# A decoder layer on one core: the first modulation and the first ten units of the input projection, by chunks of 128 features

## The chip, the core and the metric

The kernel runs on one core of a Trainium2 chip, as one launch. Its time is the device time in microseconds, and the number to compare is the median of several executions. The engines are TensorE (PE), VectorE (DVE), ScalarE (ACT), GpSimd (POOL) and SyncE (SP); PEld is TensorE's weight load. The work of each engine is written out by hand, and the engines wait for each other on semaphores.

## What is computed

One layer over 256 tokens of 1024 features. A vector c gives six modulation rows, of which the first two (shift and scale) act on the normalised input:

```python
mod = silu(c) @ w_ada + b_ada                   # w_ada: 1024 x 6144
sh1, sc1, g1, sh2, sc2, g2 = split(mod, 6)
h = rms_norm(x, g_pre_mix) * (1.0 + sc1) + sh1
proj = h @ w_in                                 # queries, keys, values of three attentions, index heads, gates
y = merge(attention_sb, attention_moba, attention_dsa, gates) @ w_o
x = x + g1 * rms_norm(y, g_post_mix)
h = rms_norm(x, g_pre_ffn) * (1.0 + sc2) + sh2
x = x + g2 * rms_norm((silu(gate) * up) @ w_down, g_post_ffn)
```

Products with weights are done as three products of a high and a low part, so each weight and each h is cut in two: high part by ScalarE, the rest by VectorE.

## The kernel before

**Blocks and units.** w_in is loaded in blocks of columns (`MIX_BLOCKS`) into two buffers `raw`, cut into `whi` and `wlo` (`cut_hi` L625, `cut_lo`, its line L923), and multiplied by units: a unit is one tile of 128 output columns, or of one half of the tokens for value blocks. There are 51 units (`mix_units` L73). Units 0 to 9 belong to blocks 0 to 3: index keys with weights, four tiles of index queries, two of queries and two of keys of the second attention, and the last heads of both. Units 10 and 11 are its values, 12 to 17 queries and keys of the first attention, 18 and 19 its values, 20 to 26 the third attention, 27 to 50 the gates. A unit runs over the 8 chunks of 128 features with three matmuls each (`three`, L1259 to L1261), into one of two PSUM banks, and ScalarE copies it out (`take_unit` L682).

**The first modulation.** SyncE loads c, x, the bias and gain vectors, and then the first 2048 columns of w_ada in six transfers with 8 KB in a row. `first_products` multiplies them chunk by chunk with silu(c) (L1266). VectorE copies the rows out (L1005), TensorE turns them (L1299), VectorE makes the shift and scale columns (L975, L979). x has been scaled by its inverse root and turned meanwhile (L1316); VectorE and ScalarE modulate it, chunk by chunk, and cut it (L1030, L733, L737, L1038). Only then unit 0 starts.

**What else is hung on the units.** All engines walk the same list of units in the same order. At unit u, VectorE does the low parts of the next block (`PIECES_AT`), index logits, parts of the softmax, rounds of the top-k search (units 25 to 32), and at the units in `ADA_UNIT` one of 16 steps of the second and third modulation: GpSimd loads 1 MB of w_ada into `ada_part`, which lies in the buffer of the modulated x, and VectorE adds it, times a column of silu(c), to `acc` (`accumulate`, L999; L993 and L996 for the first of eight). GpSimd loads part n+1 once VectorE is through with part n (`load_part` L542); there is one buffer. Head n of the 16 is scored behind unit `HEAD_START` + 2n, exponentiated one unit later, normalised by VectorE at the next, and turned or summed by TensorE behind the third. Index logits are made in pairs of heads behind units 5, 7, 9 and 11. GpSimd masks the scores once all are added.

## Time and profile before

| | us |
|---|---|
| median of three runs | 473.8 (473.58 to 475.11) |
| profiled execution | 475.17 |
| its span | 473.0 |

| engine | busy us | share |
|---|---|---|
| TensorE | 441.7 | 93% |
| VectorE | 317.1 | 67% |
| ScalarE | 237.7 | 50% |
| GpSimd | 55.0 | 12% |

The span is the stretch from the first to the last instruction of one execution; its time is that of the whole launch, 2.2 us more. Times in rows are from the span's start. A row of a timeline gives start, duration, engine, line, operation, output and inputs, shapes and count; in brackets is the idle time of the engine before it and who ended it. Matmuls overlap in a pipeline: the distance between starts tells their pace, not the duration.

### The profile page before, as it was taken

Reading aid. Unit: us, or ns where it says so; the run is one execution under the profiler, and the core shown is the slowest. Engines: PE = TensorE matmul, PEld = TensorE weight load, DVE = VectorE, ACT = ScalarE, POOL = GpSimd, SP = SyncE. Lnnn points to the kernel's source line nnn. Section 1 sums busy time; section 2 is a strip of 40 time slices with the busy share of each in tenths; the row PEclk is TensorE's granted clock in tenths of the full one; section 3 lists DMA queues with packets and bytes.
Section 4 is the critical chain, followed back from the end, with each engine's and each line's share of the span. In section 5 each row is a group of like instructions: output and inputs, shape, how many; then the busy total and the mean of one; then the engine's idle time right before and its main releaser. Section 6 shows DMA issues by size and latency. Waiting matters only on the chain.

```text
span 473.0 us, 7656 instructions
## 1 busy us (share of the span) xinstructions
PE 441.7 (93%) x2927; PEld 389.7 (82%) x2927; DVE 317.1 (67%) x542; ACT 237.7 (50%) x417; POOL 55.0 (12%) x84
## 2 busy tenths in 40 slices
PE   0959999999999999999979999999999999999994
PEld 0529999999889989998977799888888888888883
DVE  3047678768399959673789547785855675585545
ACT  6046555647576655657547237554454253445232
POOL 2001001200023140000399100000000000000000
PEclk9958999999999999999999999999999999999998
DMA  8996888596955675742667910997475646620002
GB/s 299 424 367 212 290 303 292 178 307 216 346 184 187 254 267 187 268 156 81 202 214 276 372 72 2 327 361 265 143 236 177 190 165 204 236 93 1 1 0 89
DMA packets 56817, 99.85 MB, mean 211 GB/s; under 512 B 5212, under 2 KB 41684, under 8 KB 53716
## 3 DMA queue, kind: packets, MB, share of 16 engines
q1 hardware_dynamic: 54132, 81.62, 50.4%
q0 software_dynamic: 2656, 17.84, 10.7%
q8 instruction: 19, 0.31, 0.3%
q14 instruction: 10, 0.08, 0.0%
HBM read 98.39 MB, written 1.06 MB: 210 GB/s over the span
## 4 chain that ended last, share of the span: by engine, by line
PE 88%; DMA 4%; DVE 3%; issue 2%; ACT 1%; SPq 1%; DVEq 0%; ACTq 0%; PEldq 0%
PE psum L1259 19%; PE psum L1260 17%; PE psum L1261 17%; PE psum L1559 16%; PE psum L1560 8%; DMA ada_end<-in_w_ada_dram 4%; PE psum L1523 3%; PE psum L1410 1%; PE psum L1349 1%; PE psum L1347 1%; PE psum L1381 1%; DVE wlo L923 1%; PE psum L1392 1%; PE psum L1316 1%; DVE acc L999 0%
## 5 line engine op out<-in xcount | busy, mean ns | idle before, releaser
L1559 PE MATMUL psum<-hcut,whi 128*128 128x512 f32 x320 | 111.7, 394 | 0.0
L1259 PE MATMUL psum<-hcut,whi 128*128 128x256 f32 (+1 forms) x360 | 106.3, 295 | 3.2 <-DVE hcut L1038 2.7
L1260 PE MATMUL psum<-hcut,whi 128*128 128x256 f32 (+1 forms) x360 | 102.9, 286 | 0.0
L1261 PE MATMUL psum<-hcut,wlo 128*128 128x256 f32 (+1 forms) x360 | 102.9, 286 | 0.0
L923 DVE TENSOR_TENSOR wlo<-raw,whi 128x1024 fp32r<-128x1024 f32 (+4 forms) x84 | 78.9, 967 | 24.9 <-ACT whi L634 24.6
L1560 PE MATMUL psum<-hcut,wlo 128*128 128x256 f32 x320 | 88.8, 277 | 0.0
L1259 PEld LDWEIGHTS psum<-hcut,whi 128*128 128x128 f32 (+1 forms) x360 | 69.4, 193 | 8.0 <-issue 3.2
L634 ACT ACTIVATE whi<-raw 128x1024 fp32r<-128x1024 f32 (+4 forms) x84 | 66.3, 821 | 16.5 <-DMA raw<-in_w_in_dram 16.5
L1559 PEld LDWEIGHTS psum<-hcut,whi 128*128 128x128 f32 x320 | 60.0, 188 | 14.1 <-issue 0.2
L1260 PEld LDWEIGHTS psum<-hcut,whi 128*128 128x128 f32 (+1 forms) x360 | 69.4, 193 | 0.0
L1261 PEld LDWEIGHTS psum<-hcut,wlo 128*128 128x128 f32 (+1 forms) x360 | 69.3, 192 | 0.0
L1560 PEld LDWEIGHTS psum<-hcut,wlo 128*128 128x128 f32 x320 | 60.1, 188 | 0.4
L1188 DVE TENSOR_TENSOR dlo<-draw,dhi 128x2048 fp32r<-128x2048 f32 x11 | 25.1, 2292 | 43.7 <-ACT dhi L832 43.7
L1183 DVE TENSOR_TENSOR wlo<-raw,whi 128x1024 fp32r<-128x1024 f32 x40 | 47.1, 1221 | 4.6 <-ACT whi L825 4.6
L825 ACT ACTIVATE whi<-raw 128x1024 fp32r<-128x1024 f32 x40 | 39.8, 1046 | 3.2 <-DMA raw<-in_w_up_dram 3.2
L832 ACT ACTIVATE dhi<-draw 128x2048 fp32r<-128x2048 f32 x11 | 20.9, 1912 | 30.8 <-PE psum L1261 30.8
L999 DVE SCALAR_TENSOR_TENSOR acc<-xn,csil,acc 128x2048 f32<-128x2048 f32 x14 | 32.9, 2350 | 4.9 <-DMA xn<-in_w_ada_dram 4.8
L870 ACT ACTIVATE fsil<-fsil 128x256 f32<-128x256 f32 x20 | 8.4, 418 | 52.8 <-DVE fsil L1200 52.8
L1260 PE MATMUL psum<-dlo,fhi 128*128 128x512 f32 x88 | 34.3, 390 | 0.0
L1259 PE MATMUL psum<-dhi,fhi 128*128 128x512 f32 x88 | 34.3, 390 | 0.0
L1261 PE MATMUL psum<-dhi,flo 128*128 128x512 f32 x88 | 34.3, 390 | 0.0
L1260 PE MATMUL psum<-wlo,hcut 128*128 128x320 f32 (+2 forms) x80 | 27.8, 347 | 0.0
(180 smaller groups left out, 695.7 us busy)
## 6 DMA issues: line engine op xcount, KB each, us to landing
raw<-in_w_up_dram SPq DMA_DIRECT2D x22, 1024.0 KB, 7.6
xn<-in_w_ada_dram POOLq DMA_DIRECT2D x16, 1024.0 KB, 5.2
raw<-in_w_in_dram SPq DMA_DIRECT2D x7, 2048.0 KB, 8.5
draw<-in_w_down_dram SPq DMA_DIRECT2D x11, 1024.0 KB, 5.0
raw<-in_w_in_dram SPq DMA_DIRECT2D x4, 1280.0 KB, 6.7
raw<-in_w_in_dram SPq DMA_DIRECT2D x3, 1536.0 KB, 6.9
raw<-in_w_ada_dram SPq DMA_DIRECT2D x2, 2048.0 KB, 9.7
ada_end<-in_w_ada_dram SPq DMA_DIRECT2D x4, 1024.0 KB, 16.9
```

The lines of the kernel that those rows point to most:

```text
L634: act.activation(block_view(whi[b % 2], b)[0:p, chunks, cols], block_view(raw[r % 2], b)[0:p, chunks, cols], ACT.Copy).then_inc(w_hi, 1)
L825: act.activation(block_view(whi[slot], B_FFN)[:, 2 * q:2 * q + 2, :], block_view(raw[slot], B_FFN)[:, 2 * q:2 * q + 2, :], ACT.Copy).then_ ...
L832: act.activation(dhi[slot][:, :, :], draw[slot][:, :, :], ACT.Copy).then_inc(d_hi, 1)
L923: dve.tensor_tensor(block_view(wlo[b % 2], b)[0:p, chunks, cols], block_view(raw[r % 2], b)[0:p, chunks, cols], block_view(whi[b % 2], b)[ ...
L999: ins = dve.scalar_tensor_tensor(acc[:, :], ada_part, csil[:, k:k + 1], acc[:, :], ALU.mult, ALU.add)
L1183: dve.tensor_tensor(block_view(wlo[slot], B_FFN)[:, 2 * q:2 * q + 2, :], block_view(raw[slot], B_FFN)[:, 2 * q:2 * q + 2, :], block_view(w ...
L1188: dve.tensor_tensor(dlo[slot][:, :, :], draw[slot][:, :, :], dhi[slot][:, :, :].bitcast(F32), ALU.subtract).then_inc(d_lo, 1)
L1259: pe.matmul(dst, a[0], b[0], start=first, stop=False)
L1260: pe.matmul(dst, a[0], b[1], start=False, stop=False)
L1261: return pe.matmul(dst, a[1], b[0], start=False, stop=last)
L1559: pe.matmul(dst[:, :], wh, hcut[:, k, :, :].rearrange("p a s -> p (a s)"), start=k == 0, stop=False)
L1560: mm = pe.matmul(dst[:, S:2 * S], wl, hhi[:, k, :], start=False, stop=k == KC - 1)
```

## The change

The first modulation is computed for one chunk of 128 features at a time, and each chunk's part of units 0 to 9 follows at once. For chunk k SyncE loads the shift and scale columns of that chunk from all rows of w_ada (two transfers, 512 bytes in a row, into one of three buffers) and the chunk's 128 rows of the 1224 columns of blocks 0 to 3 (three transfers). `row_products` makes the modulation row of the chunk, ScalarE copies it, `turn_row` turns it into two columns, VectorE adds bias and gain, multiplies the raw transposed x by scale and inverse root, ScalarE adds the shift and cuts, VectorE makes the rest. The ten units then take three matmuls each, into ten half banks side by side, which stay open over all eight chunks. The row products of chunk k+1 stand behind the first of the ten units of chunk k, its turn behind the fourth. x is turned unscaled, by transposes; both inverse roots are computed in one chain of two columns, spread to a row and multiplied in. ScalarE takes the ten units after the last chunk. The bias and gain vectors are loaded by ScalarE's queue. From unit 10 on the old form goes on, with all four pairs of index logits behind units 10 to 13, heads one unit later (`HEAD_START` 14) and the sixteen steps of the later modulation at other units.

```diff
+FIRST_BLOCK, FIRST_UNIT = 4, 10
+Q_COLS, CHUNK_COLS = W_IX + HD + H_IX, W_IX + HD + H_IX + 2 * W_MB
+CHUNK_BASE = [W_IX, 0, Q_COLS, Q_COLS + W_MB - HD]
...
-HEAD_START = 13
+HEAD_START = 14
...
+LOGIT_PAIR_AT = {FIRST_UNIT + j: j for j in range(H_IX // 2)}
...
-ADA_UNIT = [2, 4, 6, 9, 12, 15, 18, 22, 25, 28, 31, 34, 37, 40, 43, 46]
+ADA_UNIT = [11, 13, 15, 17, 19, 21, 23, 25, 27, 30, 32, 34, 37, 40, 43, 46]
...
+        ada = [sb(f"ada{i}", [P, KC, 2, P], scope=start) for i in range(3)]
+        end_raw, end_hi, end_lo = [[sb(f"end_{name}{i}", [P, CHUNK_COLS], dt, scope=start) for i in range(2)]
+                                   for name, dt in (("raw", F32), ("hi", F32R), ("lo", F32R))]
...
+        def chunk_view(bufs, ends, k):
+            if k >= 6:
+                return ends[k - 6][:, :]
+            return bufs[k // 3][:, CHUNK_COLS * (k % 3):CHUNK_COLS * (k % 3 + 1)]
+        def first_place(u):
+            return bank[u // 2][:, S * (u % 2):S * (u % 2 + 1)]
+        def mod_turned_col(k):
+            return bank[6 + k % 2][:, 2 * k:2 * k + 2]
...
+            def load_chunk(k):
+                if k >= 3:
+                    sp.wait_ge(gemv, k - 2)
+                for a in range(2):
+                    sp.dma_start(ada[k % 3][:, :, a, :], ada_dram[:, :, D * a + P * k:D * a + P * (k + 1)]).then_inc(ada_in[k], 16)
+                view = chunk_view(raw, end_raw, k)
+                sp.dma_start(view[:, 0:Q_COLS], in_dram[:, k, O_QIX:O_QIX + Q_COLS]).then_inc(chunk_in[k], 16)
+                heads = in_dram[:, k, O_QMB:O_QMB + 2 * W_MB].rearrange("p (a n) -> p a n", a=2)
+                pairs, last = view[:, Q_COLS:CHUNK_COLS - P], view[:, CHUNK_COLS - P:CHUNK_COLS]
+                sp.dma_start(pairs.rearrange("p (a n) -> p a n", a=2), heads[:, :, 0:W_MB - HD]).then_inc(chunk_in[k], 16)
+                sp.dma_start(last.rearrange("p (a n) -> p a n", a=2), heads[:, :, W_MB - HD:W_MB]).then_inc(chunk_in[k], 16)
+            def load(b):
+                dst, arrived = raw[b % 2], raw_in[b % 2]
+                if b < FIRST_BLOCK + 2:
+                    sp.wait_ge(w_hi, 6 * (b - FIRST_BLOCK + 1))
+                    sp.wait_ge(w_lo, 6 * (b - FIRST_BLOCK + 1))
+                else:
+                    sp.wait_ge(w_hi, 4 * (b - 1))
+                    sp.wait_ge(w_lo, 4 * (b - 1))
...
-                    pool.wait_ge(h_lo, 4)
+                    pool.wait_ge(tmp_ready, KC)
...
+            for k in range(KC):
+                act.wait_ge(chunk_in[k], 48)
+                act.activation(chunk_view(whi, end_hi, k), chunk_view(raw, end_raw, k), ACT.Copy).then_inc(w_hi, 2)
+                act.wait_ge(gemv, k + 1)
+                if k >= 2:
+                    act.wait_ge(mod_turned, k - 1)
+                act.activation(mrow[:, S * (k % 2):S * (k % 2 + 1)], bank[5][:, 0:S], ACT.Copy).then_inc(row_kept, 1)
+                act.wait_ge(tmp_ready, k + 1)
+                act.activation(hhi[:, k, :], htmp[k % 2], ACT.Identity, bias=col[0][:, k:k + 1]).then_inc(chunk_hi, 1)
+                if k == 1:
+                    act.preload_act_table_set("natural_log_exp_and_others")
             for q in range(4):
...
+                cut_hi(FIRST_BLOCK, q)
...
+            for u in range(FIRST_UNIT):
+                take_unit(u)
+            for u in range(FIRST_UNIT, N_UNITS):
...
+            v2, r2, t2 = var[:, 0:TT], rinv[:, 0:TT], root_[:, 0:TT]
+            then(dve.reciprocal(r2, t2))
+            then(dve.tensor_tensor(t2, v2, r2, ALU.mult))
+            then(dve.tensor_tensor(t2, t2, r2, ALU.mult))
+            then(dve.tensor_scalar(t2, t2, -0.5, 1.5, ALU.mult, ALU.add))
+            dve.tensor_tensor(r2, r2, t2, ALU.mult).then_inc(root_ready, 1)
+            dve.wait_ge(root_turned, 1)
+            dve.tensor_copy(rootrow, bank[3][:, S:2 * S]).then_inc(rootrow_ready, 1)
+            def chunk_cut_lo(k):
+                dve.wait_ge(w_hi, 2 * (k + 1))
+                dve.tensor_tensor(chunk_view(wlo, end_lo, k), chunk_view(raw, end_raw, k),
+                                  chunk_view(whi, end_hi, k).bitcast(F32), ALU.subtract).then_inc(w_lo, 2)
+            def chunk_columns(k):
+                dve.wait_ge(mod_turned, k + 1)
+                shift, scale = mod_turned_col(k)[:, 0:1], mod_turned_col(k)[:, 1:2]
+                then(dve.scalar_tensor_tensor(col[0][:, KC + k:KC + k + 1], scale, vecs[:, VEC_ADA + KC + k:VEC_ADA + KC + k + 1],
+                                              vecs[:, VEC_PRE_MIX + k:VEC_PRE_MIX + k + 1], ALU.add, ALU.mult))
+                then(dve.tensor_tensor(col[0][:, k:k + 1], shift, vecs[:, VEC_ADA + k:VEC_ADA + k + 1], ALU.add))
+                dve.sem_inc(mod_ready, 1)
+                if k == 0:
+                    dve.wait_ge(rootrow_ready, 1)
+                if k % 4 < 2:
+                    dve.wait_ge(x_kept_act, k // 4 + 1)
+                else:
+                    dve.wait_ge(x_kept_dve, k // 4 + 1)
+                if k >= 2:
+                    dve.wait_ge(chunk_hi, k - 1)
+                dve.scalar_tensor_tensor(htmp[k % 2], h32[:, k, :], col[0][:, KC + k:KC + k + 1], rootrow,
+                                         ALU.mult, ALU.mult).then_inc(tmp_ready, 1)
+            def chunk_rest(k):
+                dve.wait_ge(chunk_hi, k + 1)
+                dve.scalar_tensor_tensor(hlo[:, k, :], htmp[k % 2], col[0][:, k:k + 1], hhi[:, k, :].bitcast(F32),
+                                         ALU.add, ALU.subtract).then_inc(chunk_lo, 1)
+            for k in range(KC):
+                if k:
+                    chunk_cut_lo(k)
+                chunk_columns(k)
+                if k == 0:
+                    chunk_cut_lo(0)
+                chunk_rest(k)
+            dve.sem_inc(col_ready, 1)
             for q in range(4):
...
+                cut_lo(FIRST_BLOCK, q)
...
+            def row_products(k):
+                pe.wait_ge(ada_in[k], 32)
+                if k == 0:
+                    pe.wait_ge(c_ready, 2)
+                else:
+                    pe.wait_ge(row_kept, k)
+                w = ada[k % 3]
+                for half in range(2):
+                    for j in range(4):
+                        mm = pe.matmul(bank[5][32 * j:32 * j + 32, 0:S], crep[:, 4 * half + j, :],
+                                       w[:, 4 * half + j, :, :].rearrange("p a n -> p (a n)"),
+                                       start=half == 0, stop=half == 1, tile_position=(0, 32 * j))
+                mm.then_inc(gemv, 1)
...
+            def turn_row(k):
+                pe.wait_ge(row_kept, k + 1)
+                if k == 0:
+                    pe.wait_ge(pick_ready, 1)
+                if k < 2:
+                    pe.wait_ge(x_kept_dve, 1)
+                else:
+                    pe.wait_ge(mod_ready, k - 1)
+                if k == 0:
+                    pe.wait_ge(x_kept_act, 1)
+                for a in range(2):
+                    mm = pe.matmul(mod_turned_col(k)[:, a:a + 1], mrow[:, S * (k % 2) + P * a:S * (k % 2) + P * (a + 1)], pick[:, :],
+                                   start=True, stop=True)
+                mm.then_inc(mod_turned, 1)
+            def turn_raw_x(i):
+                for t in range(TT):
+                    if i == 0:
+                        pe.wait_ge(x_in[t], 16)
+                    for c in (2 * i, 2 * i + 1):
+                        mm = pe.transpose(turned(c)[:, P * t:P * (t + 1)], xt[:, t, P * c:P * (c + 1)], ident[:, :])
+                mm.then_inc(x_raw_turned, 1)
+            def first_unit(u, k):
+                b, what, c0, n, dest = UNITS[u]
+                base = CHUNK_COLS - P if what == "last head" else CHUNK_BASE[b] + c0
+                wh, wl = [chunk_view(x, ends, k)[:, base:base + n] for x, ends in ((whi, end_hi), (wlo, end_lo))]
+                dst = first_place(u)[0:n, :]
+                pe.matmul(dst, wh, hhi[:, k, :], start=k == 0 and u in (1, 2, 4, 6, 8), stop=False, skip_group_check=True)
+                pe.matmul(dst, wh, hlo[:, k, :], start=False, stop=False, skip_group_check=True)
+                return pe.matmul(dst, wl, hhi[:, k, :], start=False, stop=k == KC - 1, skip_group_check=True)
...
+            for i in range(4):
+                turn_raw_x(i)
             pe.wait_ge(vec_in, 16 * 6)
-            pe.transpose(bank[0][:, 0:VEC_END], vec_rows[:, :], ident[0:VEC_END, 0:VEC_END]).then_inc(vec_turned, 1)
+            pe.transpose(bank[4][:, 0:VEC_END], vec_rows[:, :], ident[0:VEC_END, 0:VEC_END]).then_inc(vec_turned, 1)
+            row_products(0)
+            pe.wait_ge(root_ready, 1)
             for t in range(TT):
-                turn_x(0, t)
-            first_products()
-            turn_rows(0)
-            for u in range(N_UNITS):
+                mm = pe.transpose(bank[3][:, S + P * t:S + P * (t + 1)], rinv[:, t:t + 1].to_broadcast([P, P]), ident[:, :])
+            mm.then_inc(root_turned, 1)
+            turn_row(0)
+            for k in range(KC):
+                pe.wait_ge(w_hi, 2 * (k + 1))
+                pe.wait_ge(w_lo, 2 * (k + 1))
+                pe.wait_ge(chunk_hi, k + 1)
+                pe.wait_ge(chunk_lo, k + 1)
+                for n in range(FIRST_UNIT):
+                    u = n ^ 1 if k == 0 and n < 2 else n
+                    if k == 0 and n == 0:
+                        pe.wait_ge(x_kept_act, 2)
+                    if k == 0 and u == 2:
+                        pe.wait_ge(x_kept_dve, 2)
+                    if k == 0 and u == 6:
+                        pe.wait_ge(rootrow_ready, 1)
+                    if k == 0 and u == 8:
+                        pe.wait_ge(vec_ready, 1)
+                    mm = first_unit(u, k)
+                    if k == KC - 1:
+                        mm.then_inc(units, 1)
+                    if n == 0 and k < KC - 1:
+                        row_products(k + 1)
+                    if n == 3 and k < KC - 1:
+                        turn_row(k + 1)
+                if k < KC - 1:
+                    mm.then_inc(chunk_done, 1)
+            for u in range(FIRST_UNIT, N_UNITS):
```

## Rows read from the trace of the kernel before

**Rows 1.** page, part 1: busy us, share of the span, instructions

```profile
PE 441.7 (93%) x2927; PEld 389.7 (82%) x2927; DVE 317.1 (67%) x542; ACT 237.7 (50%) x417; POOL 55.0 (12%) x84
```

**Rows 2.** timeline of the start, all engines

```profile
6.11 0.63 ACT L648 ACTIVATE xn<-xt 128x512 f32<-128x512 f32 x1 [0.59 <-DMA xt<-in_x_dram]
...
27.01 1.94 PE L1266 MATMUL psum<-ada_end,crep 128*32 128x512 f32 x8 [1.57 <-DMA ada_end<-in_w_ada_dram]
...
29.85 1.11 PE L1299 MATMUL psum<-ident,mrow 128*128 128x128 f32 x4 [0.91 <-DVE mrow L1005]
...
33.66 0.46 PE L1259 MATMUL psum<-hcut,whi 128*72 128x256 f32 x1 [2.70 <-DVE hcut L1038]
```

**Rows 3.** stretches: length, busy (instructions) per engine, granted clock, DMA share, GB/s

```profile
15.00:20.00 5.00, 5.00 (x46) 3.08 (x49) 0.00 (x0) 0.00 (x0) 0.00 (x0) 1.00 1.01 428
36.00:38.00 2.00, 2.00 (x12) 2.00 (x11) 1.57 (x2) 2.00 (x4) 0.69 (x1) 0.50 0.04 13
39.00:40.00 1.00, 1.00 (x9) 1.00 (x8) 1.00 (x2) 1.00 (x2) 0.00 (x0) 0.74 0.70 246
150.00:160.00 10.00, 10.00 (x82) 9.43 (x81) 9.82 (x20) 6.21 (x10) 2.84 (x8) 1.00 0.87 304
```

**Rows 4.** timeline of TensorE: products, first unit, logits, end of the tenth unit

```profile
17.30 3.64 PE L1266 MATMUL psum<-raw,crep 128*32 128x512 f32 x32
...
34.14 0.41 PE L1261 MATMUL psum<-hcut,wlo 128*72 128x256 f32 x1
...
34.35 0.41 PE L1259 MATMUL psum<-hcut,whi 128*72 128x256 f32 x1
...
54.02 0.49 PE L1347 MATMUL psum<-qk 64*128 64x128 f32 x4
...
54.87 0.38 PE L1259 MATMUL psum<-hcut,whi 128*128 128x256 f32 x1
...
67.62 0.49 PE L1347 MATMUL psum<-qk 64*128 64x128 f32 x4
```

**Rows 5.** DMA packets, at 47 to 48, then at 45 to 46.5

```profile
DMA packets 938, 0.31 MB, mean 311 GB/s; under 512 B 912, under 2 KB 931, under 8 KB 931
...
q1 hardware_dynamic: 931, 0.25, 119.4%
...
DMA packets 462, 0.59 MB, mean 394 GB/s; under 512 B 0, under 2 KB 462, under 8 KB 462
```

**Rows 6.** groups of instructions by form: count, busy us, mean ns, idle before

```profile
L634 ACT ACTIVATE whi<-raw 128x1024 fp32r<-128x1024 f32 x28 | 28.9, 1050 | 0.0
...
L812 ACT ACTIVATE hcut<-xn 128x256 fp32r<-128x256 f32 x8 | 3.3, 418 | 14.6 <-POOL xn L607 14.6
...
L1064 DVE SCALAR_TENSOR_TENSOR score<-bufp,wix,score 128x256 f32<-128x256 f32 x7 | 3.4, 480 | 0.0
...
L1523 PE MATMUL psum<-xn,raw 128*128 128x128 f32 x128 | 14.7, 276 | 0.7 <-ACT xn L665 0.7
```

**Rows 7.** parts of the later modulation: landing, issue, sum; GpSimd's mask

```profile
DMA to landing us min/median/max: 4.9/5.2/7.3
...
55.34 0.53 POOL L548 DMA_DIRECT2D xn<-in_w_ada_dram  x1 [9.44 <-DVE acc L999]
...
60.28 2.35 DVE L999 SCALAR_TENSOR_TENSOR acc<-xn,csil,acc 128x2048 f32<-128x2048 f32 x1 [0.59 <-DMA xn<-in_w_ada_dram]
...
81.42 3.23 POOL L566 TENSOR_SCALAR_AFFINE_SELECT score<-score 128x128 f32<-128x128 f32 x2 [8.48 <-DVE score L1064]
```

**Rows 8.** timeline: takes of units 17 and 27, VectorE between

```profile
95.48 0.38 ACT L697 ACTIVATE qk<-psum 128x256 f32<-128x256 f32 x1 [0.83 <-PE psum L1261]
...
127.28 0.56 DVE L1095 SCALAR_TENSOR_TENSOR bufp<-psum,bufa 128x384 f32<-128x384 f32 x1 [4.68 <-ACT bufa L754]
...
129.40 2.36 DVE L923 TENSOR_TENSOR wlo<-raw,whi 128x1024 fp32r<-128x1024 f32 x2 [0.97 <-ACT whi L634]
...
137.80 0.47 ACT L706 ACTIVATE qk<-psum,vecs 128x256 f32<-128x256 f32 x1 [1.38 <-PE psum L1261]
```

More of the change, by code:

```diff
@@ L88, in mix_units @@
     features(2, T_QMB, W_MB - HD)
-    keys(3, T_QMB, T_KMB, W_MB)
+    features(3, T_KMB, W_MB - HD)
+    units.append((3, "last head", W_MB - HD, P, (T_QMB + W_MB // P, T_KMB + W_MB // P)))
     tokens(4, "values", 0, W_MB, V_MB)
@@ L181, in pieces_at @@
     plan = {}
-    for b in range(N_MIX):
+    for b in range(FIRST_BLOCK, N_MIX):
         us = [n for n, u in enumerate(UNITS) if u[0] == b]
@@ L210 @@
     0, 3 * KC, 9 * KC, 10 * KC, 11 * KC, 12 * KC, 13 * KC)
-SIGMOID_FROM = max(EXP_AT) + 4
+SIGMOID_FROM = max(EXP_AT) + 3
 EARLY_GATES = SIGMOID_FROM - FIRST_GATE
 SIGMOID_BATCHES = 3
-def raw_uses():
-    uses = [("ada", u) for u in range(2)]
-    uses += [("block", b) for b in range(B_FFN)]
-    return uses
-RAW = raw_uses()
-N_RAW = len(RAW)
+N_RAW = B_FFN - FIRST_BLOCK
 LOADS = {b: 1 for b in range(B_FFN)}
@@ L232, in raw_arrivals @@
 def raw_arrivals():
-    count, out = [0, 0], []
-    for r, (kind, b) in enumerate(RAW):
-        count[r % 2] += 16 * (1 if kind == "ada" else LOADS[b])
-        out.append(count[r % 2])
+    count, out = [0, 0], {}
+    for b in range(FIRST_BLOCK, B_FFN):
+        count[b % 2] += 16 * LOADS[b]
+        out[b] = count[b % 2]
     return out, count
 RAW_ARRIVED, RAW_COUNT = raw_arrivals()
-RAW_OF_BLOCK = {b: r for r, (kind, b) in enumerate(RAW) if kind == "block"}
 def decoder_layer(nc, x, c, w_ada, b_ada, g_pre_mix, g_post_mix, w_in, b_gate, w_proj_sb,
@@ L560, in _ @@
             load_part(0)
[L561 to L562 removed]
+            for u in range(FIRST_UNIT, N_UNITS):
+                if u == max(LOGIT_PAIR_AT):
                     pool.wait_ge(score_added, TT * H_IX)
@@ L683, in take_unit @@
                 b, what, c0, n, dest = UNITS[u]
-                src = bank[B_UNIT + u % 2]
-                act.wait_ge(units, u + 1)
+                src = first_place(u) if u < FIRST_UNIT else bank[B_UNIT + u % 2]
+                act.wait_ge(units, 2 * (u // 2) + 2 if u < FIRST_UNIT else u + 1)
                 if what == "index keys and weights":
@@ L731, in _ @@
-            for pair in range(4):
-                c = 2 * pair
-                act.activation(h32[:, c, :], turned(c), ACT.Identity, bias=col[0][:, c:c + 1],
-                               scale=col[0][:, 8 + c:9 + c]).then_inc(h_act, 1)
-                act.wait_ge(h_act, pair + 1)
-                act.wait_ge(h_dve, pair + 1)
-                act.activation(hhi[:, 2 * pair:2 * pair + 2, :], h32[:, 2 * pair:2 * pair + 2, :], ACT.Copy).then_inc(h_hi, 1)
-            for u in range(N_UNITS):
+            act.wait_ge(x_in[0], 16)
@@ L1024, in _ @@
[L1024 to L1039 removed]
+            dve.wait_ge(ident_ready, 1)
@@ new lines, in _ @@
+            dve.tensor_reduce(pick[:, :], ident[:, :].rearrange("p (a b) -> p a b", b=32)[:, :, 0], AX_X, ALU.add).then_inc(pick_ready, 1)
+            dve.wait_ge(x_in[1], 16)
+            dve.tensor_tensor_reduce(squares0[1], xt[:, 1, :], xt[:, 1, :], 1.0, 0.0, ALU.mult, ALU.add,
+                                     ssq[:, 0, 1:2]).then_inc(ss_ready, 2)
+            for i in (1, 3):
+                dve.wait_ge(x_raw_turned, i + 1)
+                dve.tensor_copy(h32[:, 2 * i:2 * i + 2, :], turned_two(i)).then_inc(x_kept_dve, 1)
@@ new lines, in _ @@
+            dve.wait_ge(vec_turned, 1)
+            then(dve.tensor_copy(vecs[:, :], bank[4][:, 0:VEC_END]))
+            dve.wait_ge(ss_ready, 4)
+            then(dve.tensor_scalar(var[:, 0:TT], ssq[:, 0, :], 1.0 / D, EPS, ALU.mult, ALU.add))
+            dve.sem_inc(var_ready, 2)
+            then(dve.tensor_scalar(vecs[:, VEC_ADA + KC:VEC_ADA + 2 * KC], vecs[:, VEC_ADA + KC:VEC_ADA + 2 * KC], 1.0, None, ALU.add))
+            dve.sem_inc(vec_ready, 1)
+            dve.wait_ge(sqrt_ready, 2)
```

256 lines of the change are left out of this document (96 added, 160 removed).

## The prediction

> **What bounds the kernel now.** Read the busy shares first: TensorE is busy 93% of the span, VectorE 67% [rows 1]. Then the timeline of the start, because the change is there: x has landed at 6.11, the last products of the first modulation end at 28.95, waiting for their weights, and the first unit's matmul starts only at 33.66 [rows 2]. Until then the DMA engines run without a gap (428 GB/s, share 1.01 at 15 to 20 us [rows 3]), so the first 29 us are bound by 8 MB of modulation weights, and 4.7 us more by a serial chain. From 33.66 on TensorE has almost no idle time until the merge. So a microsecond of unit work moved ahead of 33.66 is a microsecond won, unless TensorE must then wait for someone later.
>
> **The reference point.** Units 0 to 9 are the same in both kernels. In before the tenth ends at 67.62 [rows 4], with two of four pairs of index logits already done by then (units 5 and 7). A pair costs 54.87 - 54.02 = 0.85, with its restart 0.9. Without them and 0.2 for two small transposes the ten units would end at 67.6 - 1.8 - 0.2 = 65.6. In after, all logits come behind the tenth unit. The question is when that end comes.
>
> **Start of after.** x is in at about 6.1. Sixteen raw transposes of x (0.23 each by the four at 29.85 [rows 2]) take until about 9.8, the vectors' transpose follows. Sums of squares and root: now one chain for both token tiles, some eight tiny operations at 0.2 behind the copies of x; I put it at 10 to 12, its two transposes and the copy at 13. The load of chunk 0 is 1.05 MB of modulation weights and 0.63 MB of w_in. The trace has no 512-byte packets in bulk: 256-byte ones (nearly all of the 931 on queue 1 at 47 to 48) move 0.25 MB in about 0.9 us, 280 GB/s, those of 1280 bytes 394 [rows 5]. In time per packet 512 bytes lie nearer the small ones; I take 325, ends 280 and 394. A chunk is then 3.2 + 1.7 = 4.9 us (ends 4.3 and 5.5); chunk 0 lands near 11.0, chunk 7 near 45.5 (ends 41 and 50). Behind chunk 0: ScalarE's cut of 1224 columns at 1050 ns per 1024 is 1.25 [rows 6], the row's copy 0.35, turn 0.6, columns 0.5, product 0.48; then VectorE's low part of the chunk (two of 1024 columns take 2.36 [rows 8]), 1.45, and of h, 0.45 [rows 6]. 11.0 + 5.3 = 16.3 for TensorE's first unit matmul.
>
> **The chunk loop.** Per chunk 30 matmuls at 0.12 (82 in the 10 us at 150 to 160 [rows 3]) = 3.6; 8 x 3.6 = 28.8. They are before's own matmuls: nothing is added. Added in between, 7 times: the row products of the next chunk (in before 32 records take 3.64 [rows 4] and eight make one of the eight rows of products, so 0.9; after has half the columns and twice the records per eighth, the same streaming) and turn_row, four records at 115 ns (14.7 us for 128) and a wait, 0.6 [rows 6]. In before these products lie under the DMA and cost nothing; here they stand in TensorE's order: 7 x 1.5 = 10.5. Clock: in before TensorE is at its 1.2 GHz level from the sparse stretch before 33.66 until about 39.5 (0.50 granted at 36 to 38, 0.74 in the second at 39; spacing 0.21, from 34.14 to 34.35, against 0.12 [rows 3, 4]). After 10 us with little work (11 to 16) I expect the same again, 5.8 us at half speed = 2.9. Sum: 16.3 + 28.8 + 10.5 + 2.9 = 58.5.
>
> Does anything else set the chunk's period of 5.1? DMA, 4.9, runs ahead and isn't late even at its upper end. ScalarE has 2.0, VectorE 2.9 per chunk. The serial chain after turn_row (columns 0.45, product 0.48, ScalarE's bias and cut 0.42, VectorE's rest 0.45, four hand-overs of 0.05 to 0.15) is 2.1 to 2.3 against 2.2 of units 4 to 9 that cover it. It just about fits; I add 1.1 over the loop (ends 0 and 5). The table load at chunk 1 fits in ScalarE's slack. **End of the tenth unit: 59.6, that is 6.0 earlier** (ends 1 and 9: no cold clock and an early start on one side, 0.7 per chunk of slip on the other).
>
> **Behind the loop: what gives it back.** SyncE's loads of blocks 4 and 5 are queued behind chunk 7 and land before 57, the takes of ten units (12 ScalarE operations, 4.5 us) run beside units 10 and 11, whose waits need only banks 0 and 1. Logits in pairs at 10 to 13 are the same work as before. I cost these at 0; uncovered, the takes could cost 2.
>
> Not free is the later modulation. In before sixteen parts of 1 MB are taken up at units 2, 4, 6, 9, 12, 15, 18, 22, every three units; in after only from unit 11, every second one: 11, 13, ..., 27. There is one buffer, so a part's cycle is: 2.35 for the sum on VectorE, 0.3 until GpSimd's issue, 5.2 to landing (min 4.9, max 7.3): 7.85; the pair 55.34 to 60.28 shows it with VectorE waiting for the DMA [rows 7]. Two feature units take TensorE 48 x 0.12 = 5.8 plus attention, some 7.2 where no value units lie. VectorE works in order: what is queued behind the waiting sum are softmax norms and low parts of the weights, and TensorE waits for both.
>
> Walk it, with T the end of the tenth unit. At unit 13 VectorE is through the logits at T+18.7, GpSimd masks the scores first (3.23 us [rows 7]) and issues part 2 at T+22.1; it lands at T+27.3. VectorE reaches it at T+24.5 and waits. Its norm of head 0, behind it, comes at T+31.3, while TensorE is ready for that head's transposes, behind unit 17, at T+29.75 (two value units at 3.5 by their 320 columns, six feature units at 3.0, four logit pairs, a score pair): 1.6 lost. Parts 3 to 6 follow every 7.85, part 7 behind the first top-k round, its sum ending at T+69.8; the third piece of the first gate block then is ready at T+70.9, against T+67.0 when TensorE reaches it unhindered (the ten units 18 to 27 take 95.4 to 137.7 in before [rows 8], less 1.4 for the sum over parts and 1.6 for heads that come later in after, and 1.5 before the unit's end): 3.9 lost, the first 1.6 in it. With 0.2 for the fourth piece: **4.1 back.** Price per us of landing time: about 5 us, as five landings stand in a row. From unit 27 on VectorE is full (9.82 of 10 us at 150 to 160 [rows 3]) and has 3 us more to do up to unit 34 than before; but it starts block 11's low part some 6 earlier than 129.40 [rows 8], so this costs nothing more. From unit 35 on both kernels are alike but for the heads one unit later; with the last output at unit 49 of 50, I put it at 0 (ends -0.5 and +1).
>
> **Sum:** 6.0 - 4.1 = 1.9 saved. Against the profiled execution (475.17, span 473.0, 2.2 outside it) 473.3; the median shown, 473.8, is 1.4 below that execution, so 471.9.
>
> **Rivals.** *A, the parts come late.* Queue 1's blocks and the parts share the DMA engines; in after they collide more often. For it: the landing of 7.3 in before. Against: 5.2 in the median. At 6.3 on average for five landings: 5 x 1.1 = 5.5 more, 477.4. The mechanism is VectorE's wait for part_in ahead of the norms; it decides from a landing of 5.6 (1.9 / 5 above 5.2) to slower than before. *B, nothing is given back.* If VectorE's lag is hidden (TensorE needs a piece only when it reaches it), the six stay: 467.8. For it: VectorE idles 4.68 us before 127.28 in before [rows 8]. *C, the chunk loop is slower than the sum:* transfers of 512 bytes at 200 GB/s would make 7.0 per chunk, chunk 7 landing at 60 and the tenth unit at 68: 473.8 + 8.4 - 6.0 + 4.1 = 480.3. For it speaks nothing in rows 5. *D, a cold loop:* if TensorE waits in each chunk and the granted clock stays at 0.50, as it did at 36 to 38, the loop costs 8 x 3.6 more less the 2.9 counted, 26 us: near 498. The Trainium skill (TensorE: Matmul & The Clock Gate, HAM oscillation) describes just such loops over K tiles, in which the wait for each tile throttles the engine anew. Against it: the sum above leaves hardly any wait inside the loop; 0.03.
>
> **Chances.** Forecast (470 to 474) 0.5; A 0.27; B 0.15; C and others of the loop 0.05; D 0.03. About 0.3% (1.4 us) can be told from no change: so faster is B, 0.28 of the forecast's half and a little of C's opposite, 0.45; same 0.31; slower 0.24. Range for 8 in 10: 467.8 to 477.8; the forecast's own is 470 to 474.
>
> **What would show it.** First unit matmul at 15 to 18 (before 33.66); 0.50 granted there for about 6 us; ten matmul groups per chunk at a period of 5.1 to 5.4; tenth unit's end at 58 to 61. VectorE waiting for DMA of xn at units 15 to 23, 2 to 3 us each; TensorE idle before a p transpose (L1392's like) at unit 17 and before the first gate block. Wrong if the row products wait for ada, if VectorE shows no wait for xn (then B), or if the span before the tenth unit's end is over 64.

## The result and the profile after

The changed kernel takes 489.55 us (median of 4 runs, 486.49 to 491.51) against 474.46 (4 runs, 473.58 to 475.17): ratio 1.0307, 95% interval 1.028 to 1.0333. It is slower by some 15 us; the forecast was 471.9 in a range of 467.8 to 477.8. The profiled execution is the fastest of the four, 486.49 with a span of 484.8, so the two profiles differ by 11.8 us in span, and the profile accounts for that much of the 15. The other three show a mean granted clock of 0.975 to 0.981 instead of 0.995.

Page of after, busy time per engine: the shares are those of before [rows 1] within 1%. TensorE's busy time is 7.8 us longer, VectorE's 6.1; the shares alone don't tell where.

```profile
PE 449.5 (93%) x3005; PEld 392.7 (81%) x3005; DVE 323.2 (67%) x554; ACT 238.7 (49%) x412; POOL 52.8 (11%) x84
```

The timeline of the start of after (start, duration, engine, line, operation, idle time and its releaser):

```profile
11.11 1.93 PE L1341 MATMUL psum<-ada,crep 128*32 128x256 f32 x16 [1.05 <-DMA ada<-in_w_ada_dram]
13.03 1.22 ACT L758 ACTIVATE whi<-raw 128x1224 fp32r<-128x1224 f32 x1 [1.69 <-DMA raw<-in_w_in_dram]
18.75 0.55 PE L1377 MATMUL psum<-hcut,whi 128*128 128x256 f32 x1 [3.15 <-DVE hcut L1095]
19.10 0.42 PE L1378 MATMUL psum<-hcut,whi 128*128 128x256 f32 x1
19.31 0.41 PE L1379 MATMUL psum<-hcut,wlo 128*128 128x256 f32 x1
...
22.02 0.40 PE L1379 MATMUL psum<-hcut,wlo 128*72 128x256 f32 x1
22.24 0.31 PE L1377 MATMUL psum<-hcut,whi 128*128 128x256 f32 x1
...
22.50 0.28 PE L1379 MATMUL psum<-hcut,wlo 128*128 128x256 f32 x1
22.62 0.28 PE L1377 MATMUL psum<-hcut,whi 128*128 128x256 f32 x1
```

First unit matmul at 18.75 (before 33.66 [rows 2]). The stretches of this profile give a granted clock of 1.00 from 18 us on, but the pace doesn't agree: the matmuls start 0.21 apart until 22.24, which is before's spacing at the 1.2 GHz level [rows 4], and 0.12 apart from then on. So the first 3.5 us of the units ran at half clock here too. Then the inside of one chunk, and the last matmul of the tenth unit with the first of the eleventh:

```profile
36.24 0.48 DVE L1095 SCALAR_TENSOR_TENSOR hcut<-bufp,col,hcut 128x256 fp32r<-128x256 f32 x1 [0.58 <-ACT hcut L764]
37.35 1.07 PE L1341 MATMUL psum<-ada,crep 128*32 128x256 f32 x16
...
39.52 0.50 PE L1358 MATMUL psum<-pick,mrow 128*128 128x1 f32 x4
41.75 0.48 DVE L1095 SCALAR_TENSOR_TENSOR hcut<-bufp,col,hcut 128x256 fp32r<-128x256 f32 x1 [0.58 <-ACT hcut L764]
41.98 0.28 PE L1379 MATMUL psum<-hcut,wlo 128*128 128x256 f32 x1
42.38 0.31 PE L1377 MATMUL psum<-hcut,whi 128*72 128x256 f32 x1
...
62.34 0.28 PE L1379 MATMUL psum<-hcut,end_lo 128*128 128x256 f32 x1
62.46 0.31 PE L1327 MATMUL psum<-whi,hcut 128*128 128x320 f32 x1
```

From 36.24 to 41.75 is the chunk's period, 5.5 us. Between two chunks (41.98 to 42.38) the next matmul comes 0.40 later instead of 0.12: TensorE takes it up when VectorE's rest of h is through, at 41.75 + 0.48. The tenth unit ends at 62.5, 3.1 earlier than the 65.6 that stand for it in before; unit 17 is taken at 92.42 (before 95.48 [rows 8]), still 3.1 ahead. Where TensorE then stands idle, by the lines that it waits at:

```profile
93.90 0.55 PE L1482 MATMUL psum<-ident,bufp 128*128 128x128 f32 x3 [1.51 <-DVE bufp L1150]
111.58 0.31 PEld L1482 LDWEIGHTS psum<-ident,bufp 128*128 128x128 f32 x3 [0.87 <-DVE bufp L1150]
128.73 0.39 PE L1327 MATMUL psum<-whi,hcut 128*128 128x320 f32 x1 [2.01 <-DVE wlo L955]
137.44 0.36 PE L1327 MATMUL psum<-hcut,whi 128*128 128x256 f32 x1 [2.31 <-DVE wlo L955]
147.50 0.42 PEld L1396 LDWEIGHTS psum<-ident,mrow 128*128 128x128 f32 x4 [1.01 <-DVE mrow L1034]
172.45 0.65 PE L1500 MATMUL psum<-buft,v 128*64 128x256 f32 x4 [1.28 <-POOL buft L602]
189.37 0.65 PE L1500 MATMUL psum<-buft,v 128*64 128x256 f32 x4 [1.59 <-POOL buft L602]
```

VectorE's norm of a head (L1150) comes late behind units 17 and 21, its low parts of the last value block and of the first gate block (L955) in units 25 and 27; the turn of a group's sum stands behind 28, GpSimd's masks (L602) behind 34 and 38. What VectorE itself waited for, and the clock behind the stall at 137 (columns: length, TensorE's busy time, granted clock, DMA share, GB/s):

```profile
89.96 2.35 DVE L1028 SCALAR_TENSOR_TENSOR acc<-xn,csil,acc 128x2048 f32<-128x2048 f32 x1 [1.94 <-DMA xn<-in_w_ada_dram]
...
116.80 0.53 POOL L576 DMA_DIRECT2D xn<-in_w_ada_dram  x1 [7.17 <-DVE acc L1028]
125.49 2.35 DVE L1028 SCALAR_TENSOR_TENSOR acc<-xn,csil,acc 128x2048 f32<-128x2048 f32 x1 [5.37 <-DMA xn<-in_w_ada_dram]
125.65 2.00 ACT L662 ACTIVATE whi<-raw 128x1024 fp32r<-128x1024 f32 x2 [2.11 <-DMA raw<-in_w_in_dram]
```

```profile
136.00:138.00 2.00, 0.56 (x5) 1.00 1.25 406
138.00:140.00 2.00, 1.81 (x10) 0.58 0.82 304
140.00:142.00 2.00, 2.00 (x10) 0.56 0.94 313
142.00:144.00 2.00, 2.00 (x11) 1.00 1.02 374
```

A part issued at 116.80 lands only at 125.49, 8.7 us later, while 2 MB of w_in (ScalarE's wait at 125.65) come over the same engines. And behind a stall of 2.5 us TensorE runs at the 1.2 GHz level for some 3.4 us: 1.7 us more.

The balance of the two profiles closes at the first projection matmul, which comes 10.2 later:

```profile
234.16 0.36 PE L1327 MATMUL psum<-ohi,whi 128*128 128x256 f32 x1 [0.90 <-issue]
```

(before: 223.96). Stalls of TensorE in after, each with its weight load's wait (the 0.4 is at 138.54, right behind the one at 137.44): 1.7 + 0.9 + 2.25 + 2.5 + 0.4 + 1.0 + 1.45 + 1.75 = 11.9; half clock 1.7; less before's own one, 0.65 at 182.82; less the lead of 3.1: 9.9 of the 10.2. Behind it 0.3 comes back up to the feed-forward loop, and 1.8 are lost in it. SyncE's issues there, one step apart, first before, then after:

```profile
349.89 0.37 SPq L507 DMA_DIRECT2D draw<-in_w_down_dram  x1
366.47 0.37 SPq L507 DMA_DIRECT2D draw<-in_w_down_dram  x1
```

```profile
343.24 0.37 SPq L534 DMA_DIRECT2D draw<-in_w_down_dram  x1
360.02 0.37 SPq L534 DMA_DIRECT2D draw<-in_w_down_dram  x1
```

16.58 against 16.78 in these two; over a pair of steps 33.13 against 33.58, in a loop whose code is the same.

### The profile page after: what moved, and what is told of

The parts are those of the page before. It is cut to its first block, busy times and chain, and to the rows that moved or that the text cites. A ratio compares the mean times of both kernels' runs of the same rounds, so it can differ in the third digit from the quotient of the medians.

```text
span 484.8 us, 7882 instructions
## 1 busy us (share of the span) xinstructions
PE 449.5 (93%) x3005; PEld 392.7 (81%) x3005; DVE 323.2 (67%) x554; ACT 238.7 (49%) x412; POOL 52.8 (11%) x84
## 4 chain that ended last, share of the span: by engine, by line
PE 70%; DVE 11%; DMA 10%; issue 4%; ACT 3%; SPq 1%; POOL 1%; DVEq 0%; ACTq 0%
PE psum L1676 15%; PE psum L1327 11%; PE psum L1329 11%; PE psum L1328 11%; DMA xn<-in_w_ada_dram 9%; PE psum L1677 8%; DVE acc L1028 4%; PE psum L1640 3%; PE psum L1377 2%; DVE wlo L955 1%; PE psum L1341 1%; DMA raw<-in_w_in_dram 1%; PE psum L1378 1%; PE psum L1379 1%; PE psum L1500 1%
## 5 line engine op out<-in xcount | busy, mean ns | idle before, releaser
L1676 PE MATMUL psum<-hcut,whi 128*128 128x512 f32 x320 | 113.3, 398 | 0.0
L1677 PE MATMUL psum<-hcut,wlo 128*128 128x256 f32 x320 | 89.8, 281 | 0.0
L1327 PE MATMUL psum<-hcut,whi 128*128 128x256 f32 x280 | 82.7, 295 | 2.5 <-DVE wlo L955 2.5
L1328 PE MATMUL psum<-hcut,whi 128*128 128x256 f32 x280 | 79.4, 283 | 0.0
L1329 PE MATMUL psum<-hcut,wlo 128*128 128x256 f32 x280 | 79.4, 283 | 0.0
L955 DVE TENSOR_TENSOR wlo<-raw,whi 128x768 fp32r<-128x768 f32 (+3 forms) x68 | 66.7, 1007 | 16.5 <-ACT whi L662 16.2
L1676 PEld LDWEIGHTS psum<-hcut,whi 128*128 128x128 f32 x320 | 60.1, 188 | 14.7
L1677 PEld LDWEIGHTS psum<-hcut,wlo 128*128 128x128 f32 x320 | 60.4, 189 | 0.3
L1327 PEld LDWEIGHTS psum<-hcut,whi 128*128 128x128 f32 x280 | 53.7, 192 | 7.8 <-issue 3.4
L662 ACT ACTIVATE whi<-raw 128x768 fp32r<-128x768 f32 (+3 forms) x68 | 55.6, 848 | 6.0 <-DMA raw<-in_w_in_dram 6.0
L1328 PEld LDWEIGHTS psum<-hcut,whi 128*128 128x128 f32 x280 | 53.8, 192 | 0.0
L1329 PEld LDWEIGHTS psum<-hcut,wlo 128*128 128x128 f32 x280 | 53.7, 192 | 0.0
L1327 PE MATMUL psum<-whi,hcut 128*128 128x320 f32 (+2 forms) x72 | 25.3, 351 | 3.5 <-DVE wlo L955 2.0
```

The source lines that it names most:

```text
L662: act.activation(block_view(whi[b % 2], b)[0:p, chunks, cols], block_view(raw[b % 2], b)[0:p, chunks, cols], ACT.Copy).then_inc(w_hi, 1)
L955: dve.tensor_tensor(block_view(wlo[b % 2], b)[0:p, chunks, cols], block_view(raw[b % 2], b)[0:p, chunks, cols], block_view(whi[b % 2], b)[ ...
L1327: pe.matmul(dst, a[0], b[0], start=first, stop=False)
L1328: pe.matmul(dst, a[0], b[1], start=False, stop=False)
L1329: return pe.matmul(dst, a[1], b[0], start=False, stop=last)
L1676: pe.matmul(dst[:, :], wh, hcut[:, k, :, :].rearrange("p a s -> p (a s)"), start=k == 0, stop=False)
```

## Experiments

All medians in us; the interval is that of the ratio to before, which read 474.3 to 475.3 beside them. Runs are called by the start of their label, x1 or z4. Runs x1, x2, x5, x6, x7 and x11 leave out part of the work, to price it.

**Parts without their bytes.** `load_part` brings 64 of 2048 columns:

```
- pool.dma_start(ada_part, ada_dram[:, n % KC, ADA_COLS * (1 + n // KC):ADA_COLS * (2 + n // KC)]).then_inc(part_in, 16)
+ c0 = ADA_COLS * (1 + n // KC)
+ pool.dma_start(ada_part[:, 0:64], ada_dram[:, n % KC, c0:c0 + 64]).then_inc(part_in, 16)
```

> The changed kernel, but each of the sixteen parts of the later modulation brings only 64 of its 2048 columns (32 KB instead of 1 MB); VectorE sums over the whole buffer as before, so most of the later modulation's weights are left out. Theory W (what is lost is VectorE's waiting for the parts, with norms and low parts queued behind it): a part lands in about 2 us, no wait is left, and the gain of the first 60 us stands: 468 to 474. Rival L (the loss lies in the chunk loop, in the takes or in GpSimd's order, not in the parts): 482 or more.

483.85 (478.89 to 484.92; 1.0089 to 1.0205). Only 5.7 of 15 us come back. That speaks against theory W as the whole cause, but the run isn't clean: its parts of 32 KB landed in 2.0 to 2.2 us with nothing else under way (issued at 59.72, 94.62, 136.79), and in 4.7 to 5.2 beside a load of w_in (86.97, 100.02, 118.18). VectorE still waited for two of them, and TensorE behind the first:

```profile
91.97 2.35 DVE L1029 SCALAR_TENSOR_TENSOR acc<-xn,csil,acc 128x2048 f32<-128x2048 f32 x1 [2.87 <-DMA xn<-in_w_ada_dram]
95.91 0.82 PE L1483 MATMUL psum<-ident,bufp 128*128 128x128 f32 x3 [1.83 <-DVE bufp L1151]
```

So 5.7 is what shorter landings give, not what no landing would.

**The same traffic, nobody waiting for it**, by a second transfer of the whole megabyte to scratch memory (x2).

> As the kernel with small parts, but behind each small part the same queue also moves the whole 1 MB into scratch memory, for which nobody waits: the traffic stays, the wait goes. Most of the later modulation's weights are left out again. Theory W: 469 to 475, near the kernel with small parts. Rival C (the traffic itself costs, by making the blocks of w_in late for ScalarE and VectorE): 479 to 488, at least half of the loss still there.

483.39 (1.0149 to 1.021), the same as without the bytes. In this form (the bytes go to memory, not to the buffer) the traffic adds nothing to the median. Here too VectorE still waited for small parts, 1.7, 1.3 and 2.9 us.

**The schedule alone, in the kernel before:**

```
- ADA_UNIT = [2, 4, 6, 9, 12, 15, 18, 22, 25, 28, 31, 34, 37, 40, 43, 46]
+ ADA_UNIT = [11, 13, 15, 17, 19, 21, 23, 25, 27, 30, 32, 34, 37, 40, 43, 46]
```

> The kernel before with one line of the change: the list of units at which the parts are taken up (11, 13, 15, ... instead of 2, 4, 6, 9, ...). Theory W: the crowding of the parts alone makes the loss, so before's start plus the same waits: 486 to 493, slower than before by 12 to 18. Rival L (the new start makes the loss): 473 to 478.

482.39 (1.0138 to 1.0172): half of the loss by one line, between the two expectations. Its profile has a stall of 1.5 us at 89.38 and one of 2 us at unit 25, with 3.4 us at half clock behind it, and its feed-forward step stays 16.55:

```profile
130.00 0.38 PE L1259 MATMUL psum<-whi,hcut 128*128 128x320 f32 x1 [2.02 <-DVE wlo L923]
```

What makes the other half (heads and logits moved, blocks met at other times) wasn't tried part by part.

**Spread evenly.**

> The changed kernel with the same sixteen parts spread evenly from unit 11 to 46 (11, 13, 16, 18, 20, 23, 25, 27, 30, 32, 34, 37, 39, 41, 44, 46), so that at most three stand two units apart in a row. Theory W: a part's cycle of 7.9 us no longer beats two and a third units of 8.7 us; a third to a half of the 13 us comes back: 482 to 486. If the loss isn't the spacing: 489 as the changed kernel.

488.44 (1.0243 to 1.0288): nearly nothing. In its profile the stalls at units 17 and 25 are gone, but there is one of 2.2 at unit 22 with 6.8 us at half clock behind it, and the one of 2.5 at unit 27 stays.

**VectorE's sums narrowed** (parts whole and waited for), and **both taken away:**

```
- ... acc[:, :], ada_part, csil[:, k:k + 1], acc[:, :], ...
+ ... acc[:, 0:64], ada_part[:, 0:64], csil[:, k:k + 1], acc[:, 0:64], ...
```

> The changed kernel with whole parts (1 MB each, waited for), but fourteen of the sixteen sums of the later modulation cover only 64 of 2048 columns, so most of the later modulation is left out. Theory V (after the kernel with small parts still took 483.9, the loss is VectorE's own work: eight sums of 2.35 us more between units 10 and 27 than the kernel before has there, and everything behind them in its order): the cycle of a part falls to 5.6 us, under two units, and VectorE is relieved: 472 to 476, no stall of over 1.5 us on TensorE between units 15 and 29, and no stretch of half clock. Rival P (late blocks of w_in, GpSimd's masks): 480 to 484.

> Small parts (64 columns, 32 KB) and sums narrowed to 64 columns in fourteen of sixteen: neither the traffic nor the work of the later modulation is left, most of it is left out. Theory V: 471 to 475, like the one with whole parts and narrow sums within 1.5 us. Then what remains against the kernel before is the first 60 us (3 us gained) and the feed-forward loop (1.9 us lost in each profile of this family). Rival P: 478 or more.

479.1 (1.0056 to 1.0131) and 476.43 (1.0009 to 1.0049), above their ranges by 3.1 and 1.4. In the first VectorE waits even longer for landings than in after (5.8, 4.7 and 5.1 us at 91.65, 106.13 and 121.76), and TensorE once behind them, at unit 17; GpSimd's masks aren't late any more, and the stall at unit 27 (2.3 with the sums) has become 0.24:

```profile
93.52 0.55 PE L1482 MATMUL psum<-ident,bufp 128*128 128x128 f32 x3 [1.44 <-DVE bufp L1150]
131.76 0.36 PE L1327 MATMUL psum<-hcut,whi 128*128 128x256 f32 x1 [0.24 <-DVE wlo L955]
```

With after this makes a square: whole 489.5; small parts 483.9 (5.7 less); small sums 479.1 (10.4 less); both 476.4 (13.1 less). So the sums, VectorE's own 2.35 us each, are the larger half, and the two overlap by 3 us. (The "eight sums more" of the expectation are four: nine stand at units 11 to 27, five in before.) (Before wasn't run without its parts: 476.4 against 474.3 isn't a price of the loop, and how much of the 10.4 the sums cost in before too isn't known.)

**What sets the chunk's period.** First less to load: from the fourth chunk on one eighth of the modulation weights. Then less for TensorE: from the third chunk on half of the row products, on top of the kernel without parts.

> The changed kernel, but from the fourth chunk on only one eighth of a chunk's modulation weights is brought (the rest of the product reads what lies in the buffer, so part of the first modulation is left out): 0.76 MB per chunk instead of 1.68. Theory D (transfers of 512 bytes and their issue set the chunk's period of 5.5 us): from chunk 3 on the period falls to the chain's own, 4.9 to 5.2, and the tenth unit ends 2 to 3 us earlier; 486 to 489. Rival S (the chain over ScalarE, VectorE and TensorE sets it): the period stays 5.4 to 5.6, the time at 489.

> Like the kernel without parts (32 KB parts, narrow sums), and from the third chunk on the row products take only the first four of eight feature groups (half of that part of the first modulation is left out): six times 0.5 us less on TensorE inside the chunk loop. Theory T (TensorE's own order of 30 matmuls, products and turn fills the chunk's 5.5 us): the period falls to 5.0 from chunk 2 on, the tenth unit ends 3 us earlier, and with VectorE relieved all of it reaches the end: 473.4 (476.4 of its own base less 3.0). Rival S (the chain over ScalarE and VectorE sets the period): 5.3 to 5.5, 475.5 to 476.5.

490.28 (1.028 to 1.0373), the low parts of h 5.5 us apart as ever (36.08, 41.59, 47.09 against 36.24, 41.75, 47.24): the DMA engines don't set it. Half the products: 474.47 against 476.43 of its base, and the same events at 35.45, 40.52, 45.60, 50.63, a period of 5.05. TensorE's own order sets it, as theory T has it, but only just: behind the turn the chain over VectorE and ScalarE ends 0.3 later than the six units that cover it, and both start from the products and the turn. The median moved 2.0 of the 3.0 expected. Theory D fell, and with it my worry about transfers of 512 bytes.

x7's profile also shows the worst case at unit 17, a part that was waited for 5.64 us and what hung on it (granted clock 0.50 from 96 to 100, half clock for 6.8 us in all):

```profile
92.86 2.35 DVE L1031 SCALAR_TENSOR_TENSOR acc<-xn,csil,acc 128x2048 f32<-128x2048 f32 x1 [5.64 <-DMA xn<-in_w_ada_dram]
96.80 0.90 PE L1485 MATMUL psum<-ident,bufp 128*128 128x128 f32 x3 [4.60 <-DVE bufp L1153]
```

**Two stalls made on purpose, in before**, ahead of units 39 and 45 (TensorE waits for short chains of GpSimd memsets).

> The kernel before with two waits put in for TensorE, ahead of units 39 and 45, on short chains of GpSimd memsets: one of about 1 us, one of about 3 us. Nothing is left out. Theory K (a long stall of TensorE is followed by a stretch of some 3.4 us at half the granted clock, a short one isn't): after the short one the granted clock stays 1.00, after the long one it is 0.50 for 3 to 4 us; 474 + 1 + 3 + 1.7 = 479.5. Rival: no such stretch, 478.

484.59 (1.0197 to 1.0233). The first came out 3.0 long instead of 1 (GpSimd was still waiting to issue a part), the second 4.0, so the short one wasn't tried. Around the first:

```profile
182.56 0.39 PE L1270 MATMUL psum<-hcut,whi 128*128 128x256 f32 x1 [3.03 <-POOLq L601]
```

```profile
182.00:184.00 2.00, 1.44 (x10) 0.86 0.70 193
184.00:186.00 2.00, 2.00 (x11) 0.50 0.96 400
186.00:188.00 2.00, 2.00 (x16) 0.79 1.05 409
```

Both are followed by some 3.4 us at half clock. By their weight loads' waits 3.3 + 4.2, and 2 x 1.7 for the clock, make 10.9; the median rose by 10.2. So theory K holds for long stalls: one of 3 us costs nearly 5. The profile has a third such stretch, from 248.3 on, behind a wait of 2.0 us that this kernel didn't add: all profiles have it in the output projection (before: 1.9 at 238.74, with 1.00 granted behind it).

**Other spacing, halves, both.** Spacing: `[10, 12, 15, 17, 20, 22, 25, 28, 31, 34, 36, ... 46]`. Halves: each part in two transfers of 1024 columns, each with its own arrival, sum and release.

> The changed kernel with the parts taken up at 10, 12, 15, 17, 20, 22, 25, 28, 31 and from 34 on every second unit: seven sums before unit 28 instead of nine, the rest where VectorE is less full (after the top-k rounds of units 25 to 32). Theory V (sums of 2.35 us and waits for landing crowd VectorE between units 15 and 29): the stalls at units 17, 19, 25 and 27 shrink from 7.7 to 2 to 3 us, the half-clock stretch at unit 28 may go with them; 480 to 484. Rival: as with the even spacing, stalls move instead of going, 487 to 490.

> The changed kernel, each part as two halves of 1024 columns with arrivals, sums and releases of their own, so that a half lands while VectorE sums the other. Same work, same bytes. Theory: the waits for landing alone are worth up to 5.6 us (489.5 against 483.9 of the kernel with small parts); two halves hide about half of them: 485 to 488. If landing isn't what matters: 489 to 491 (32 operations more on VectorE, some 2 us of it).

> The changed kernel with both: parts as two halves, and taken up at 10, 12, 15, 17, 20, 22, 25, 28, 31, 34, 36, ... 46. Alone the spacing gave 483.0, the halves 483.65, against 489.5. If crowding and landing were separate causes, 477; if both shorten the same chain of VectorE behind the same stalls (units 17 to 29), less than the sum: 479.5 to 482. Either way it stays above before's 474.4.

483.0 (1.0167 to 1.0201), 483.65 (1.0158 to 1.022), both 481.4 (1.0112 to 1.0189). They overlap, as the square said. In all three TensorE still waits at unit 27: 2.3, 2.4 and 3.1. VectorE of the kernel with both, behind ScalarE's late high part:

```profile
126.76 2.36 DVE L957 TENSOR_TENSOR wlo<-raw,whi 128x1024 fp32r<-128x1024 f32 x2 [3.12 <-ACT whi L664]
...
129.67 0.61 DVE L1191 MAX8 top<-score 128x8 f32<-128x128 f32 x2
...
131.10 2.48 DVE L1031 SCALAR_TENSOR_TENSOR acc<-xn,csil,acc 128x1024 f32<-128x1024 f32 x2
133.50 2.35 DVE L957 TENSOR_TENSOR wlo<-raw,whi 128x1024 fp32r<-128x1024 f32 x2
```

A top-k round and a sum stand between the two pairs of low parts, all in the 7 us of two value units. So the last try clears units 25 and 26 of both:

> Halves as before, and VectorE kept clear at units 25 and 26, where the low part of the first gate block falls: the parts are taken up at 10, 12, 14, 16, 18, 20, 22, then 27, 30, 33, 35, 37, 39, 42, 44, 46, the eight top-k rounds at units 27 to 34 instead of 25 to 32. Theory V: the stall of 2.5 us at unit 27 and the half-clock stretch behind it (1.7 us) go: 477 to 478.5. Rival: the stall goes to another unit, 480 to 482. In neither case under before's 474.4, since the feed-forward loop keeps its 1.9 us and the loop's gain is 3.

483.41 (480.46 to 488.11; 1.0162 to 1.0281); without the longest of the four, 1.6% above the shortest, 482.3, against 481.4 of its base. The stall at 27 is gone, and two others stand at units 21 and 22 (the expectation of x9 calls the first one unit 19), behind seven sums that are now two units apart:

```profile
112.75 0.55 PE L1485 MATMUL psum<-ident,bufp 128*128 128x128 f32 x3 [1.60 <-DVE bufp L1153]
116.85 0.36 PE L1330 MATMUL psum<-hcut,whi 128*128 128x256 f32 x1 [2.13 <-DVE wlo L957]
```

The rival was right: the stall moved. No version made here beats before.

**The feed-forward loop.** Addresses, then the place of TensorE's code: 8, 20 and 44 semaphore instructions ahead of the loop, on top of the kernel with halves and spacing, and 5 on top of the last one.

> The changed kernel with its one new small buffer made 16 columns wide instead of one (64 bytes instead of 4), which moves every buffer allocated behind it. In the kernel before a step of the feed-forward loop takes 16.55 us (the start of one load of down weights to the next), in all kernels with the change 16.80, with the same instructions. Theory A (addresses): 16.55 again, and 487.5. Rival: 16.80 and 489.5, then it is something else, the place of the loop's code for one.

> The same with 8 more semaphore instructions on TensorE ahead of the feed-forward loop, nothing else. Theory place (where TensorE's loop code lies sets its pace): a step of the loop may differ from 16.80 us in one of three kernels with 8, 20 and 44 such instructions, and comes back to 16.55 in at least one. Rival: 16.80 in all three.

> The same with 20 such instructions. Theory place: 16.55 or another step than 16.80 in at least one of the three; rival: 16.80.

> The same with 44 such instructions. Theory place: 16.55 or another step than 16.80 in at least one of the three; rival: 16.80.

> The same kernel with five more semaphore instructions on TensorE ahead of the feed-forward loop. Theory place: a step of 16.55 us in the loop; rival: 16.80 again, then the place of TensorE's code isn't shown to matter and the cause stays open. Time 477 to 479, or 1.9 less.

487.71 (1.0238 to 1.0305), and single runs of 479.65, 481.07, 486.52 and 487.85. The step is 16.76 to 16.81 in all five; x3 and x12, which are before with other edits, keep 16.55 to 16.59. Neither the one move of addresses nor any of four moves of code changes it. The cause stays open. The last profile, 4 us above the median of its base, has a head's norm late at unit 21 and nearly 14 us at half clock, from 113 to 127.

```profile
114.86 0.90 PE L1485 MATMUL psum<-ident,bufp 128*128 128x128 f32 x3 [3.85 <-DVE bufp L1153]
```

```profile
114.00:118.00 4.00, 3.14 (x15) 0.50 0.00 2
...
122.00:126.00 4.00, 4.00 (x16) 0.50 1.01 352
```

## Why the prediction was wrong

- **First unit matmul at 16.3:** 18.75. The weights of chunk 0 came at 13.03 instead of 11.0, and the chain behind them took 5.7 instead of 5.3.
- **Chunk period 5.1:** 5.5. What binds it was right (TensorE's own order, with the chain all but tied; x7 and x11 show it), one term was too small: products, turn and what lies between them are 1.9 and not 1.5 per chunk (1.07 + 0.50 in the rows, and 0.3 at the chunk's end; the 1.1 put in for that was half of it). The cold clock of 2.9 came, in half its length here: by the pace of the matmuls 3.5 us from 18.75 on, and the first chunk took 7.0, 1.5 more than the others. In x6 0.50 is granted until 27.2, and the first chunk takes 9.3. Sum: 18.75 + 7.0 + 6 x 5.5 + 3.6 = 62.4 for the 59.6 forecast. **The gain was 3.1, not 6.0.**
- **Give-back of 4.1:** this is the step that failed most. Net of before's own stall it is 11.3 in TensorE's waits and 1.7 in clock. The waits at the first head and at the gate block were foreseen by place (1.6 at unit 17, measured 1.7; 3.9 in all up to the gate block, measured 7.7); those at units 21 and 25, 3.1 together, weren't. What failed is "from unit 27 on nothing more": I argued that block 11's low part starts 6 us earlier than in before. It began at 129.48 in after, against 129.40 [rows 8]: ScalarE had waited for the block's bytes until 125.65, and VectorE for a part until 125.49. The lead was gone before the crowding began, and the crowding (low parts, top-k, sums, the group's sum and turn) then cost 2.9 at unit 27, 1.0 behind 28 and 3.2 at the masks.
- **The price was put on the wrong thing.** I priced landings, and treated a sum's own 2.35 us as already in the cycle. Of before's sums three lie at units 2 to 6, where VectorE has room, and five between units 11 and 27; after has nine there, 8.3 us more (the first of each eight takes 1.3 instead of 2.35), nearly three times its lead. The square of runs gives 10.4 to the sums and 5.7 to shorter landings; x3, the new list of units alone in before, gives 7.4 to both.
- **Rival A** had its premise nearly come true: the five parts in a row (issued at 84.97 to 116.80) land after 6.0 us on average (5.0, 5.2, 6.0, 5.0, 8.7), near the 6.3 that A names, and shorter landings give back 5.7 as against its 5.5. Yet it covers 5.5 of the 17.7 us between forecast and measurement, since it takes the same 4.1 as its base. B and C are excluded by the traces (C's 200 GB/s stands in no row; the chunks' loads moved 279 to 320); D too, the loop runs at full clock from 27 us on at the latest.
- **The clock was only counted at the start.** The Trainium skill's rule named under D (TensorE: Matmul & The Clock Gate, HAM oscillation) was looked for inside the loop, where TensorE hardly waits. The rows show half clock behind single stalls in the middle of the kernel, always behind the long ones (last section). The sum had no term for that.
- **Tail 0:** 1.8 lost in a loop with unchanged code; unforeseen and unexplained.

The range ended at 477.8 because its upper end came from landings alone. The chunk loop's own saving is real (x11 carries 2.0 of what it saves to the end), but it is small beside what a displaced side job costs.

## What to carry to other kernels

When a start is shortened by letting TensorE begin early, list the side work that filled the old start on the other engines (here VectorE's first sums) and find the units that now take it: its own busy time is the price, before any wait. Walk the units where that engine has least room, not only the first ones, and check that the lead still exists when you get there: a transfer or an in-order queue may hold the block at its old time. Price a stall of TensorE of 3 us and more with what the clock takes behind it, 1.7 us and more here, and one of 2 us as a risk of the same.
